# Query, key, pooled and retention input chunks as two matmul runs of 512 and 256 columns

## What is computed

```python
def hybrid_layer(x, ...):                    # first block, twice
    x = x + 0.5 * swiglu(rms_norm(x, ffn1_norm), ffn1_w_gate_up, ffn1_w_down)
    h = rms_norm(x, mix_norm)
    u, q, k, v, gl = split(h @ w_in)         # 512, 512, 512, 512, 2048 columns
    y_pool = multiscale_pool(u, pool_w, pool_scale)
    q, k = rope(rms_norm(q, q_norm)), rope(rms_norm(k, k_norm))   # 8 heads of 64
    y_attn = moba_attention(q, k, v)
    merged = gate0 * (y_pool @ w_branch_pool) + gate1 * (y_attn @ w_branch_attn)
    x = x + merged @ w_out
    x = x + 0.5 * swiglu(rms_norm(x, ffn2_norm), ffn2_w_gate_up, ffn2_w_down)

# second block, twice:
    q_na, k_na, v_na, q_r, k_r, v_r, g_r, gate_a, gate_b = split(x @ w_in)
    ya = neighbourhood_attention(q_na, k_na, v_na, rpb)           # 8 heads of 64
    yb = bidirectional_retention(rotary(q_r), rotary(k_r), v_r, g_r, ...)  # 4 heads of 128
    # gates, w_out, layer norm, convolved GLU with w_up and w_down, layer norm
```

## Time and profile before

| | |
|---|---|
| median of 3 runs | 1954.64 us (1953.98 to 1955.01) |
| the profiled execution's own time | 1954.63 us |
| its span, first to last instruction | 1952.8 us |
| TensorE busy (matmuls) | 1940.7 us, 99% |
| weight loads | 1665.2 us, 85% |
| VectorE busy | 1363.1 us, 70% |
| ScalarE busy | 1035.5 us, 53% |
| GpSimd busy | 164.3 us, 8% |
| granted TensorE clock, mean | 0.999 |

### The profile page before, as it was taken

How to read it: one execution, slowest core, us unless ns; L and a number is a source line. 1 busy time by engine, 2 the same in 40 slices (tenths; PEclk the granted TensorE clock), 3 DMA queues, 4 the chain that set the end, 5 groups by cost and what they waited for, 6 DMA issues and landing times.

```text
span 1952.8 us, 27601 instructions
## 1 busy us (share of the span) xinstructions
PE 1940.7 (99%) x10534; PEld 1665.2 (85%) x10534; DVE 1363.1 (70%) x1652; ACT 1035.5 (53%) x1201; POOL 164.3 (8%) x152
## 2 busy tenths in 40 slices
PE   9999999999999999999999999999999999999998
PEld 8888978888888889788889978888888978888887
DVE  7666577666676666677666556577888666677887
ACT  6444555544454455655445554356556554456664
POOL 0000130000000003104002201040001301000000
PEclk9999999999999999999999999999999999999999
DMA  8555635455455546456555544564554554555552
GB/s 328 193 185 180 206 140 194 174 192 193 172 194 193 193 160 207 153 179 234 186 191 190 171 178 141 206 248 176 193 193 145 196 177 158 208 206 191 186 191 87
DMA packets 55132, 365.74 MB, mean 187 GB/s; under 512 B 6672, under 2 KB 7952, under 8 KB 12176
## 3 DMA queue, kind: packets, MB, share of 16 engines
q1 hardware_dynamic: 49680, 349.99, 50.2%
q0 software_dynamic: 1472, 9.44, 1.3%
q10 hardware_dynamic: 3904, 5.25, 1.0%
HBM read 359.40 MB, written 1.05 MB: 185 GB/s over the span
## 4 chain that ended last, share of the span: by engine, by line
PE 96%; DVE 2%; ACT 1%; DMA 1%; issue 0%; ACTq 0%; SPq 0%; DVEq 0%
PE gate_two L1693 12%; PE up_two L1693 12%; PE bank L1624 9%; PE bank L1625 9%; PE bank L1626 9%; PE gate_two L1624 8%; PE gate_two L1626 8%; PE gate_two L1625 8%; PE gate_two L1698 6%; PE up_two L1698 6%; PE up_two L1882 1%; PE bank L1851 1%; PE up_two L1866 1%; PE bank L2143 1%; DVE w_lo L1019 0%
## 5 line engine op out<-in xcount | busy, mean ns | idle before, releaser
L1019 DVE TENSOR_TENSOR w_lo<-raw,w_hi 128x2048 fp32r<-128x2048 f32 x318 | 735.0, 2312 | 246.4 <-ACT w_hi L569 240.8
L569 ACT ACTIVATE w_hi<-raw 128x2048 fp32r<-128x2048 f32 x322 | 614.6, 1909 | 95.2 <-PE bank L1626 65.5
L1693 PE MATMUL gate_two<-br_parts,w_hi 128*128 128x512 f32 x1056 | 266.5, 391 | 0.9 <-DVE w_lo L1206 0.8
L1693 PE MATMUL up_two<-br_parts,w_hi 128*128 128x512 f32 x1024 | 246.2, 391 | 0.0
L1693 PEld LDWEIGHTS gate_two<-br_parts,w_hi 128*128 128x128 f32 x1056 | 198.1, 188 | 43.3 <-issue 2.0
L1693 PEld LDWEIGHTS up_two<-br_parts,w_hi 128*128 128x128 f32 x1024 | 188.2, 188 | 37.0
L1624 PE MATMUL bank<-w_lo,hid_hi 128*128 128x512 f32 x480 | 187.5, 391 | 0.0
L1625 PE MATMUL bank<-w_hi,hid_lo 128*128 128x512 f32 x480 | 187.5, 391 | 0.0
L1626 PE MATMUL bank<-w_hi,hid_hi 128*128 128x512 f32 x480 | 186.7, 389 | 0.0
L1624 PE MATMUL gate_two<-w_lo,br_parts 128*128 128x512 f32 x448 | 179.6, 401 | 0.0
L1626 PE MATMUL gate_two<-w_hi,br_parts 128*128 128x512 f32 x448 | 174.8, 390 | 0.0
(11 more groups left out here) (274 smaller groups left out, 2958.8 us busy)
## 6 DMA issues: line engine op xcount, KB each, us to landing
raw<-stream SPq DMA_DIRECT2D x328, 1024.0 KB, 4.8
area<-rpb POOLq DMA_DIRECT2D x2, 1536.0 KB, 7.8
area<-rows POOLq DMA_DIRECT2D x3, 1024.0 KB, 5.1
raw<-stream SPq DMA_DIRECT2D x8, 256.0 KB, 7.4
softT<-area ACTq DMA_DIRECT2D x32, 64.0 KB, 5.2
area<-rows POOLq DMA_DIRECT2D x2, 768.0 KB, 4.7
konst<-consts SPq DMA_DIRECT2D x1, 1344.0 KB, 9.0
area<-xT ACTq DMA_DIRECT2D x4, 256.0 KB, 6.7
```

The lines of the kernel that those rows point to most:

```text
L569: act.activation(w_hi[:, s, :], raw[:, s, :], ACT.Copy).then_inc(hi_ready[s], 1)
L1019: dve.tensor_tensor(w_lo[:, s, :], raw[:, s, :], w_hi[:, s, :].bitcast(F32), ALU.subtract).then_inc(lo_ready[s], 1)
L1693: pe.matmul(pair[:, f, :, :], w_hi[:, s, at:at + P], parts[:, :, k, :], start=k == 0, stop=False, skip_group_check=True)
```

## The change

Chunks 0 to 3, 6 and 7 of the first block's mixer and chunks 1, 2, 3, 6, 7 and 8 of the second's go from `features` to `halves`, each with a pair of banks (`qk_pairs`, `u_pairs`, `mix2_pairs`); banks 0 and 1 become one tensor, `low_two`. ScalarE now copies the second half out and VectorE adds the first. In the first block's mixer ScalarE's square and scaled copy work on the sum in SBUF and stand behind a wait for VectorE's addition (`pair_sum`), after the swap DMAs of the chunk before and after `qk_var`; in iteration 0 they also stand behind `split_after`, and VectorE's addition stands behind its own `split_after`. For u the addition stands ahead of the scaling. In the second block VectorE's addition raises `mix_evac`. The spread of the norm factor moves to between the two runs of its chunk, in the feed-forward stages too, and always uses bank 3. Semaphores of the output are shared by engine instead of one for each pair of tiles.

```diff
--- before.py
+++ after.py
@@ -218,14 +218,19 @@
-banks = [ctx.enter_context(nc.psum_tensor(f"bank{b}", [P, 2, T], F32)) for b in range(4)]
+low_two = ctx.enter_context(nc.psum_tensor("low_two", [P, 2, 2, T], F32))
+banks = [low_two[:, 0, :, :], low_two[:, 1, :, :]]
+banks += [ctx.enter_context(nc.psum_tensor(f"bank{b}", [P, 2, T], F32)) for b in (2, 3)]
 gate_two = ctx.enter_context(nc.psum_tensor("gate_two", [P, 2, 2, T], F32))
...
 turned_x = [banks[(6, 7, 6, 7, 0, 1, 0, 1)[k]][:, k // 2 % 2, :] for k in range(DT)]
-rstd_norms = [banks[b][:, 1, :] for b in (3, 6, 3)]
+rstd_spread = banks[3][:, 1, :]
+qk_pairs = (gate_two, up_two, gate_two, up_two)
+u_pairs = (up_two, low_two)
+mix2_pairs = {1: up_two, 2: gate_two, 3: up_two, 6: low_two, 7: gate_two, 8: low_two}
 turned_m = [banks[6 + k // 2 % 2][:, k % 2, :] for k in range(DT)]
@@ -316,6 +321,8 @@
 branch_evac = signal("branch_evac", 2, 4)
+low_part = signal("low_part", 6, 6)
+pair_sum = signal("pair_sum", 6)
 qk_sq_ready = signal("qk_sq_ready", 4)
@@ -391,7 +398,7 @@
 rear_hi = signal("rear_hi", 0, 1)
-out_pair = [sem(f"out_pair{j}") for j in range(HALVES)]
+out_pair = [sem(f"out_by_{engine}") for engine in ("scalar", "vector")]
 ln_var = signal("ln_var", 0, 2 * TT)
@@ -424,7 +431,7 @@
     for j in range(HALVES):
-        sp.wait_ge(out_pair[j], 2)
+        sp.wait_ge(out_pair[j % 2], 2 * (j // 2) + 2)
         sp.dma_start(out[:, j * 2 * T:(j + 1) * 2 * T], flat(work[:, 2 * j:2 * j + 2, :])).then_inc(out_done, 16)
@@ -756,16 +763,12 @@
                 gate_out(m, 1)
-            bank = banks[4 + m % 2]
             if m == 0:
...
             if m < 4:
-                col = C_Q if m < 2 else C_K
-                act.activation(qk[:, 2 * m:2 * m + 2, :], bank[:, :, :], ACT.Copy, scale=cur[:, col:col + 1]
-                               ).then_inc(mix_evac.sem, 1)
-                if m >= 2:
-                    act.wait_ge(qk_ms.sem, here.at(qk_ms, m - 1))
-                act.activation(qk_sq[:, m % 2, :], flat(bank[:, :, :]), ACT.Square).then_inc(qk_sq_ready.sem, 1)
+                lower_half(qk[:, 2 * m:2 * m + 2, :], qk_pairs[m]).then_inc(low_part.sem, 1)
+            elif m in (6, 7):
+                lower_half(u[:, 2 * (m - 6):2 * (m - 5), :], u_pairs[m - 6]).then_inc(low_part.sem, 1)
             elif m == 5:
@@ -788,6 +791,13 @@
                 e.then_inc(qk_var_ready.sem, 1)
+            if m < 4:
+                col, some = C_Q if m < 2 else C_K, qk[:, 2 * m:2 * m + 2, :]
+                act.wait_ge(pair_sum.sem, here.at(pair_sum, m + 1))
+                if m >= 2:
+                    act.wait_ge(qk_ms.sem, here.at(qk_ms, m - 1))
+                act.activation(qk_sq[:, m % 2, :], flat(some), ACT.Square).then_inc(qk_sq_ready.sem, 1)
+                act.activation(some, some, ACT.Copy, scale=cur[:, col:col + 1]).then_inc(mix_evac.sem, 1)
             if m == 10:
@@ -889,12 +899,17 @@
                 wide_out(1, m)
-            if m < 4:
-                act.activation(qk[:, 2 * m:2 * m + 2, :], bank[:, :, :], ACT.Copy,
-                               scale=HEAD_DIM ** -0.5 if m < 2 else 1.0).then_inc(mix_evac.sem, 1)
+            if m == 0:
+                act.activation(qk[:, 0:2, :], bank[:, :, :], ACT.Copy, scale=HEAD_DIM ** -0.5).then_inc(mix_evac.sem, 1)
+            elif m < 4:
+                act.activation(qk[:, 2 * m:2 * m + 2, :], mix2_pairs[m][:, :, 1, :], ACT.Copy,
+                               scale=HEAD_DIM ** -0.5 if m == 1 else 1.0).then_inc(low_part.sem, 1)
             elif 6 <= m < 10:
                 two = ret_qk[:, 2 * (m - 6):2 * (m - 5), :]
-                act.activation(two, bank[:, :, :], ACT.Copy).then_inc(mix_evac.sem, 1)
+                if m < 9:
+                    lower_half(two, mix2_pairs[m]).then_inc(low_part.sem, 1)
+                else:
+                    act.activation(two, bank[:, :, :], ACT.Copy).then_inc(mix_evac.sem, 1)
                 if m == 6:
@@ -1008,7 +1023,7 @@
             act.activation(work[:, k, :], turned_z[k], ACT.Identity, bias=cur[:, C_B2 + k:C_B2 + k + 1],
-                           scale=cur[:, C_G2 + k:C_G2 + k + 1]).then_inc(out_pair[k // 2], 1)
+                           scale=cur[:, C_G2 + k:C_G2 + k + 1]).then_inc(out_pair[0], 1)
@@ -1062,7 +1077,7 @@
         dve.wait_ge(rstd_ready.sem, here.at(rstd_ready, n + 1))
-        dve.tensor_copy(factor[:, :], rstd_norms[n]).then_inc(factor_ready.sem, 1)
+        dve.tensor_copy(factor[:, :], rstd_spread).then_inc(factor_ready.sem, 1)
         dve.wait_ge(factor_ready.sem, here.at(factor_ready, n + 1))
@@ -1262,11 +1277,17 @@
                 split_after(here, c)
+            if m < 4:
+                dve.wait_ge(low_part.sem, here.at(low_part, m + 1))
+                add_upper(qk[:, 2 * m:2 * m + 2, :], qk_pairs[m]).then_inc(pair_sum.sem, 1)
             if m == 3:
...
             if m in (6, 7):
-                dve.tensor_tensor(u[:, 2 * (m - 6):2 * (m - 5), :], banks[4 + m % 2][:, :, :], factors, ALU.mult
-                                  ).then_inc(mix_scaled.sem, 1)
+                some = u[:, 2 * (m - 6):2 * (m - 5), :]
+                dve.wait_ge(low_part.sem, here.at(low_part, m - 1))
+                add_upper(some, u_pairs[m - 6]).then_inc(pair_sum.sem, 1)
+                dve.wait_ge(pair_sum.sem, here.at(pair_sum, m - 1))
+                dve.tensor_tensor(some, some, factors, ALU.mult).then_inc(mix_scaled.sem, 1)
             if m in (18, 19):
@@ -1400,6 +1421,17 @@
             chunk_done(here, m)
+            if m in mix2_pairs:
+                upper = mix2_pairs[m][:, :, 0, :]
+                dve.wait_ge(low_part.sem, here.at(low_part, m if m < 4 else m - 2))
+                if m == 1:
+                    some = qk[:, 2:4, :]
+                    e = dve.scalar_tensor_tensor(out=some, in0=upper, scalar=HEAD_DIM ** -0.5, in1=some, op0=ALU.mult,
+                                                 op1=ALU.add)
+                else:
+                    e = add_upper(qk[:, 2 * m:2 * m + 2, :] if m < 4 else ret_qk[:, 2 * (m - 6):2 * (m - 5), :],
+                                  mix2_pairs[m])
+                e.then_inc(mix_evac.sem, 1)
             if 0 <= m - 5 < HEADS:
@@ -1611,7 +1643,7 @@
                     dve.tensor_scalar(work[:, k, :], turned_z[k], cur[:, C_G2 + k:C_G2 + k + 1],
-                                      cur[:, C_B2 + k:C_B2 + k + 1], ALU.mult, ALU.add).then_inc(out_pair[k // 2], 1)
+                                      cur[:, C_B2 + k:C_B2 + k + 1], ALU.mult, ALU.add).then_inc(out_pair[1], 1)
@@ -1683,7 +1715,7 @@
-    def halves(c, pair, parts, k_first=None):
+    def halves(c, pair, parts, k_first=None, between=None):
@@ -1708,6 +1740,8 @@
                     both(k, f)
+            if between:
+                between()
             for k in range(DT):
@@ -1908,11 +1942,9 @@
-            def spread_at(k):
-                if k == 5:
-
-                    pe.wait_ge(rs_ready.sem, here.at(rs_ready, n + 1))
-                    spread_factor(rstd_norms[n]).then_inc(rstd_ready.sem, 1)
+            def spread_rstd():
+                pe.wait_ge(rs_ready.sem, here.at(rs_ready, n + 1))
+                spread_factor(rstd_spread).then_inc(rstd_ready.sem, 1)
@@ -1923,15 +1955,13 @@
             def start(c):
-                k_first = unscaled(n) if c == c0 else spread_at if c == c0 + 2 else None
+                k_first = unscaled(n) if c == c0 else None
+                between = spread_rstd if c == c0 + 2 else None
                 if layer == 0 and n == 0 and c < 2:
                     k_first = first_pieces(c)
-                if n == 1:
-                    features(c, two(banks[4 + (c - c0) % 2]), br_hi, br_lo, DT, k_first=k_first)
-                else:
-                    if c == c0 + 2:
-                        pe.wait_ge(gate_sum.sem, here.at(gate_sum, n // 2 * PAIRS + 1))
-                    halves(c, up_two if c == c0 + 1 else gate_two, br_parts, k_first)
+                if n != 1 and c == c0 + 2:
+                    pe.wait_ge(gate_sum.sem, here.at(gate_sum, n // 2 * PAIRS + 1))
+                halves(c, up_two if c == c0 + 1 else gate_two, br_parts, k_first, between)
                 if c == c0 + 1 and layer == 0 and n == 0:
@@ -1943,10 +1973,14 @@
-            if 2 <= m < 8:
-                pe.wait_ge(mix_evac.sem, here.at(mix_evac, m - 1))
+            if 2 <= m < 5:
+                pe.wait_ge(pair_sum.sem, here.at(pair_sum, m - 1))
+            elif m == 6:
+                pe.wait_ge(pair_sum.sem, here.at(pair_sum, 4))
+            elif m == 7:
+                pe.wait_ge(qk_var_ready.sem, here.at(qk_var_ready, 4))
             elif m == 8:
-                pe.wait_ge(mix_scaled.sem, here.at(mix_scaled, 1))
+                pe.wait_ge(mix_evac.sem, here.at(mix_evac, 6))
             elif m in (10, 12, 14):
@@ -1960,11 +1994,10 @@
                 wide_tokens(c, m % 2, (banks[4], banks[5]), br_hi, br_lo, wide_half,
```

(11 more changed lines are left out.)

## The result

The changed kernel took 1961.97 us (median of 6 runs, 1960.90 to 1964.06), the kernel before 1954.74 (6 runs). The ratio is 1.0037, 95% interval 1.0027 to 1.0048: slower by 0.4%, near the forecast of 1962.0. The profiled execution took 1961.85 us, with a span of 1960.0.

What follows compares the result with a forecast made beforehand. TensorE, busy 1940.7 of 1952.8 us, bounds the kernel. First block 1.6 + 1.8 and 1.6 + 1.2, second 2 x 0.6, together +7.4 us, gains included, on 1954.63: 1962.0 us, range 1959 to 1966.

Steps and rivals of the forecast that it cites:

- the gain: TensorE, 24 changed chunks: a pair is cheaper than three products by 0.19 us a chunk, 4.6 us in all.
- the third place: Second block's chunks 7 and 8: ScalarE's swaps wait for VectorE's addition, transposes 1.2 us late, net +0.6 us a layer.
- the first place: Start of the first block's mixer: TensorE waits 2.3 us for chunk 0's square after chunk 1, +1.6 us a layer.
- The second place: First block, scores after chunk 7: the addition delays u and the softmax; +0.8 + 1 and +0.2 + 1 us.
- Rival 3: In the mixers the pair is no cheaper than three products; the waits stand, 1966.6 us, chance 0.07.
- the gap formula: Skill's isolated matmul gap, N/2.4 + 2.5 ns: three narrow 328 ns, pair 325, so a gain of only 1.0 us.
- term d: First block, after chunk 7: how much later the swap lands; between 0 and 2.3 us, taken as 1.
- Rival 1: All waits are covered and the gain stands: 1950.0 us, chance 0.10.
- Rival 2: Only the first place holds; swaps land early and the second block's exponents have room: +0.2, 1954.8 us, chance 0.25.

Runs made afterwards that it cites:

- The fills: 8 or 18 unused matmuls in TensorE's wait for chunk 0's square: on the changed kernel 1961.57 or 1963.81 us; 8 with only the start's pairs left, 1958.01 us.
- the second block's order: Changed kernel with VectorE adding the halves before the left-over remainder in the second block's iterations 7 and 8: 1961.54 us.
- the start alone: Changed kernel with pooled inputs and second block's chunks 6 to 8 in old form, chunk 0's addition still behind the remainder: 1962.30 us, once more 1963.72.
- The version without any of the three places: Changed kernel with chunk 0's addition ahead of slot 0's remainder, pooled inputs and second block's chunks 6 to 8 in old form: 1951.90 us, again 1951.91.
- the order at the start: VectorE's order in the first block's iteration 0; with chunk 0's addition moved ahead of slot 0's remainder, nothing else, the changed kernel took 1955.31 us.

## Why the prediction was right, and where it was wrong

The number is in part luck: the gain and the third place held, but the forecast for the first place was 2.8 us too low and that for the second 2.6 too high.

**The gain** was right: 0.39 us for two chunks, 0.58 for three, 0.19 each. Rival 3 (no cheaper in the mixers) is out, and so is the gain of 1.0 us in all by the gap formula of the Trainium skill (TensorE: Matmul & The Clock Gate, Back-to-back issue gap). The formula gives 2.5 ns a tile, not the prediction's 2.7, and 1.0 us either way; likewise two chunks' gain takes 12.49 to 12.11, not 12.05, and nothing hangs on it.

**The first place**: the wait was right, 2.09 us against 2.3, the mean squares 1.90 late against 1.96, its releaser and its chain as worked out. The step that failed is the one after it: "Chunks 2 and 3 give back 0.19 each, so the mean squares of 220.33 come 1.6 late." They gave that back, but chunk 2 took some 1.6 us longer at half the clock. The prediction counted an idle time as its own length. The fills show the rest: with TensorE kept busy for as long, granted clock 1.00 and no slow chunk. The Trainium skill (TensorE: Matmul & The Clock Gate, Part 1: The HAM clock gate) says that an idle TensorE falls to 1.2 GHz; the windows of 0.57 agree. The prediction did not weigh it. By that page alone, though, a wait of 2.09 us need not have brought the fall, and the traces show it behind 6 of 10 such waits.

**The second place** was wrong: forecast +1.8 and +1.2 us, measured 0.0 and +0.4. The term d was set to 1 in a range whose lower end, 0, was argued by "nothing in the change makes it shorter". It was shorter: the swap landed 8.60 after chunk 5's end instead of 9.35, VectorE no longer waited for it, and the next remainder began at 11.40 (248.33 less 236.93) instead of 12.08. These 0.7 us paid for the 0.78 of the addition. Why the swap landed sooner is not shown. In layer 2 the transposes came 0.39 later, counted from the end of chunk 5, near the 0.23 of the prediction at d = 0. The Trainium skill (DMA: Bandwidth & Descriptors, Queues, rings and completion order) has each DMA engine take its queues in turn; from that the prediction worked out a d near 0, which is the better number, but for another reason. In these traces the swaps don't pass the load: 2.0 us without it, 5.0 to 5.6 behind it.

**The third place** was right in its times. In the changed kernel, the swap after chunk 8 and the last weights of head 3:

```profile
1124.01 1.28 ACTq L685 DMA_DIRECT2D area<-area  x2
```

```profile
1127.47 0.62 DVE L1195 TENSOR_SCALAR soft<-soft,stat 128x256 f32<-128x256 f32 x2
```

The scores after chunk 5 had moved by 5.80 us (1093.47 to 1099.27). Less that, the swap was at 1118.2, forecast 1118.4, and the weights, ready at 1128.1, at 1122.3, forecast 1122.6. The transposes came 1.0 and 0.9 us late by this count, forecast 1.2; TensorE's idle time of 1.16 and 1.18 is longer because it contains what chunks 6 to 8 had gained. The cause was only in part what the prediction named: with ScalarE's swaps freed by the second block's order, 0.8 of the 1.2 us of idle time stayed, and only with chunks 6 to 8 in their old form was all of it gone.

**The rivals.** Rival 1 (all covered) is out. Rival 2 (only the start, 1954.8) is out as a time, for the start alone is 1962.3, but it has the second place better than the forecast: the swaps did land early, and the place cost next to nothing. The version without any of the three places took 1951.9, 0.14% below the kernel before, and what its remaining 14 pairs should give is 14 x 0.19 = 2.7 us. Measured are 2.7 and 3.1 in two batches, with an interval of 1.0 to 4.5. The changed kernel lies 10.1 us above it: 6.7 by the order at the start, 2.7 by the second block's chunks 6 to 8 and 0.7 by the pooled inputs, each net of its chunks' gain. That account hangs on the order in which the three are undone: with the other two gone, the start alone costs 10.4 us and not 6.7. Part of the difference goes with the lower clock of its longer executions, whose places were not seen; the rest stays open.

## What to carry to other kernels

When an evacuation goes from one engine to two, each addition enters an order written for less work: look in that order for the long operation just ahead of it (here a 2.29 us remainder), and move the short one forward, unless it only exchanges places with another that someone waits for. Where the engine has no room left in the iteration (here 6.5 us of work in 7.3), a new order may only move the wait, and the change belongs in those chunks that have room. And an idle time of TensorE can cost more than its length: read the granted clock in the stretch behind it, in more than one execution.
